# The value products of two attentions: one piece or two halves among the first jobs

## The reference

```python
def moba_nsa_mixer(h, w_in, w_out, rel_bias, cmp_pos_k, ...):       # layer 0: "first attention", EVEN
    mq, mk, mv, nq, kc, vc, ksl, vsl, kwn, vwn, gz = _split(hp @ w_in, EVEN_SPLITS)
    ...
    # 8 heads attend to their block of 256 keys, 8 more have three branches
    p_cmp = masked_softmax(s_cmp, ...); o_cmp = p_cmp @ v_cmp       # compressed keys
    o_slc = p_s @ v_s                                               # selected blocks
    o_win = p_w @ v_w                                               # window
    o_b = g[..., 0:1] * o_cmp + g[..., 1:2] * o_slc + g[..., 2:3] * o_win   # g = sigmoid(gz)
    return concat(o_a, o_b) @ w_out

def fox_mixer(h, w_in, b_forget, w_out):                            # layer 1: "second attention", ODD
    q, k, v, fz = _split(h @ w_in, ODD_SPLITS)
    cum = jnp.cumsum(jax.nn.log_sigmoid(fz + b_forget))
    p = masked_softmax(q @ k.T * scale + cq - cum, causal)
    return (p @ v) @ w_out                                          # 16 heads of 64
```

## Time and profile before

| | |
|---|---|
| time, median of 3 runs | 1239.46 us (1237.42 to 1242.24) |
| the profiled execution | 1237.19 us, of which its span 1235.4 us |
| PE busy | 1192.0 us (96% of the span), 7770 instructions |
| PEld busy | 1046.7 us (85%) |
| DVE busy | 825.7 us (67%) |
| ACT busy | 658.1 us (53%) |
| POOL busy | 236.0 us (19%) |
| granted TensorE clock | 0.995, in the mean |
| DMA | 205.56 MB in the span, mean 166 GB/s |

### The profile page before, as it was taken

How to read it: one execution, slowest core, us unless ns; L and a number is a source line. 1 busy time by engine, 2 the same in 40 slices (tenths; PEclk the granted TensorE clock), 3 DMA queues, 4 the chain that set the end, 5 groups by cost and what they waited for, 6 DMA issues and landing times.

```text
span 1235.4 us, 19213 instructions
## 1 busy us (share of the span) xinstructions
PE 1192.0 (96%) x7770; PEld 1046.7 (85%) x7770; DVE 825.7 (67%) x1267; ACT 658.1 (53%) x1074; POOL 236.0 (19%) x300
## 2 busy tenths in 40 slices
PE   7898999999999999999999999999999899999996
PEld 6786788888888688888888889999997698888996
DVE  5957776666586686675657777457865757667643
ACT  6428666643343756664346655336546754655531
POOL 4104421210000431220012222000004511212101
PEclk9999999999999999999999999999999899999999
DMA  7791245455444335455544554652451122455451
GB/s 281 253 240 35 102 171 197 181 202 204 173 171 194 148 105 202 174 201 205 190 171 153 202 182 152 205 213 105 171 205 69 35 103 104 170 197 178 158 196 56
DMA packets 33800, 205.56 MB, mean 166 GB/s; under 512 B 3744, under 2 KB 6320, under 8 KB 12720
## 3 DMA queue, kind: packets, MB, share of 16 engines
q1 hardware_dynamic: 30416, 200.47, 45.4%
q10 hardware_dynamic: 3296, 3.87, 1.6%
HBM read 202.87 MB, written 1.46 MB: 165 GB/s over the span
## 4 chain that ended last, share of the span: by engine, by line
PE 77%; DVE 13%; ACT 5%; DMA 2%; issue 1%; ACTq 0%; POOL 0%; POOLq 0%; DVEq 0%
PE ps L669 36%; PE ps L674 23%; PE ps L672 5%; PE ps L673 5%; DVE wl L611 4%; DMA e_bt<-scratch 2%; DVE tf L2228 1%; ACT wh L582 1%; PE ps L693 1%; PE ps L695 1%; PE ps L694 1%; DVE y L1949 1%; ACT pb L924 1%; DVE xb L747 1%; ACT pb L923 1%
## 5 line engine op out<-in xcount | busy, mean ns | idle before, releaser
L611 DVE TENSOR_TENSOR wl<-raw,wh 128x2048 fp32r<-128x2048 f32 (+2 forms) x194 | 420.4, 2172 | 148.3 <-ACT wh L582 148.3
L669 PE MATMUL ps<-xb,wh 128*128 128x512 f32 x1424 | 500.7, 397 | 4.6 <-DVE wl L611 4.1
L674 PE MATMUL ps<-xb,wl 128*128 128x256 f32 x1696 | 475.6, 280 | 0.0
L582 ACT ACTIVATE wh<-raw 128x2048 fp32r<-128x2048 f32 (+2 forms) x196 | 352.1, 1799 | 151.1 <-PE ps L674 112.9
L669 PEld LDWEIGHTS ps<-xb,wh 128*128 128x128 f32 x1424 | 267.3, 188 | 70.3 <-issue 5.7
L674 PEld LDWEIGHTS ps<-xb,wl 128*128 128x128 f32 x1696 | 321.6, 190 | 0.0
L674 PE MATMUL ps<-ab,wl 128*128 128x256 f32 x1088 | 305.7, 281 | 0.0
L669 PE MATMUL ps<-ab,wh 128*128 128x512 f32 x640 | 225.1, 397 | 0.1
L674 PEld LDWEIGHTS ps<-ab,wl 128*128 128x128 f32 x1088 | 206.4, 190 | 0.0
L669 PEld LDWEIGHTS ps<-ab,wh 128*128 128x128 f32 x640 | 120.1, 188 | 29.2 <-DVE ab L982 0.8
L866 DVE TENSOR_TENSOR tf<-ps,tf 128x256 f32<-128x256 f32 x148 | 61.8, 421 | 117.7 <-ACT tf L861 117.5
(11 more groups left out here) (324 smaller groups left out, 1324.7 us busy)
## 6 DMA issues: line engine op xcount, KB each, us to landing
raw<-wstream SPq DMA_DIRECT2D x162, 1024.0 KB, 4.8
raw<-wstream SPq DMA_DIRECT2D x32, 704.0 KB, 4.1
e_bt<-scratch ACTq DMA_DIRECT2D x16, 128.0 KB, 8.8
o_bt<-scratch SPq DMA_DIRECT2D x2, 1024.0 KB, 9.9
raw<-wstream SPq DMA_DIRECT2D x2, 560.0 KB, 8.8
raw<-wstream SPq DMA_DIRECT2D x4, 256.0 KB, 6.5
h<-xt ACTq DMA_DIRECT2D x4, 256.0 KB, 7.7
raw<-wstream SPq DMA_DIRECT2D x2, 512.0 KB, 9.7
```

Source lines behind the costliest of these rows:

```text
L582: e.g.activation(WH[i % HLN][:, 0:w], RAW[i % RAWN][:, 0:w], ACT.Copy).then_inc(S["hi"], 1)
L611: e.g.tensor_tensor(WL[q][:, 0:w], RAW[i % RAWN][:, 0:w], f32(WH[q][:, 0:w]), ALU.subtract).then_inc(S["lo"], 1)
L669: e.g.matmul(PS[b][:, :].rearrange("p (a t) -> p a t", a=2), wh[:, sl], x2[:, :, cs], start=start, stop=k == p.nk - 1, skip_group_check=pair)
L674: ins = e.g.matmul(o, wl[:, sl], xh[:, cs], start=False, stop=k == p.nk - 1, skip_group_check=pair)
```

## The change

What it does, by part:

- **First attention, PE.** `ev1` is done in two halves: chunk 14 in step 2 and chunk 15 in step 5, with scores 4 and 5 and turns 0 and 1 between them. Its outputs are in banks 1 and 0 (`fixed=(1, 0)`), those of the `pv` products.
- **First attention, ACT.** The high half of chunk 16 stands before exp 2; the copies of `ev1` and the gate exps stand in step 5 behind exp 5.
- **First attention, DVE.** The low half of chunk 16 stands in step 5, behind max 5, reciprocal 3 and the copy of turn 1. The factors' block of six instructions in steps 7 and 9 is cut in three: `dve_even_sums` in steps 1 and 2, `dve_even_gates` in 6 and 7, `dve_even_weights` in 8 and 9, with a semaphore `pcs` between them.
- **Second attention, PE.** `ov1` is done in two halves in steps 2 and 5 of the attention, into banks 1 and 0; `ov0` has banks 5 and 6.
- **Second attention, ACT and DVE.** The high half of chunk 65 stands in step 3, its low half in step 4; the copies of `ov1` behind exp 5. The quarters of chunk 66 move to ACT's steps 7, 9, 11, 13 and DVE's 14 to 17.
- **Banks.** Three products have no place in the ring any more, so later products take other banks than before.

The order in which SP fetches, and POOL's, are the same. The diff (the list of semaphores, which gains `pcs`, left out; so is the removal of `ov1` in front of the second attention on ACT and PE where a line only goes away):

```diff
@@ -290,7 +290,7 @@
         Gemm("kc", "small", 1, 0, 0, "ev_dve"), Gemm("vc", "small", 1, 0, 0, "ev_dve"),
         Gemm("ev0", "toks", 512, 8, 4, "ev_act"),
         Gemm("cs0", "small", 1, 0, 0, "ev_dve"), Gemm("cs1", "small", 1, 0, 0, "ev_dve"),
-        Gemm("ev1", "toks", 280, 8, 4, "ev_act"),
+        Gemm("ev1", "toks", 280, 8, 4, "ev_act", fixed=(1, 0)),
         Gemm("even", "attention", 0, 0, 0, ""),
         Gemm("eo", "cols", 8, 8, 16, "h_eo", fixed=(3, 4), wide=True),
         Gemm("up0", "cols", FF, 8, 16, "ev_dve", wide=True),
...
-        Gemm("ov0", "toks", 512, 8, 4, "ev_act"), Gemm("ov1", "toks", 512, 8, 4, "ev_act"),
+        Gemm("ov0", "toks", 512, 8, 4, "ev_act", fixed=(5, 6)), Gemm("ov1", "toks", 512, 8, 4, "ev_act", fixed=(1, 0)),
...
-        def pe_toks(e, p, ready):
+        def pe_toks(e, p, ready, part=slice(None)):
...
-            for _, k, c, at, fresh, signals in p.blocks:
+            for _, k, c, at, fresh, signals in p.blocks[part]:
...
@@ -1143,8 +1143,9 @@
             A = EVEN
             for i in range(A.n + 4):
                 if i == 2:
-                    act_exp_biased(e, A, 2)
-                    act_exp_biased(e, A, 3)
+                    hi_to(e, G["eo"].first)
+                if i == 5:
+                    act_exp_biased(e, A, 5)
                     act_gemm(e, G["ev1"], drain=act_toks(G["ev1"], e_v, 512, 0), ahead=1)
                     for tb in range(2):
                         gz = e_v[tb][:, 768:792]
@@ -1152,7 +1153,7 @@
                         e.g.activation(gz, gz, ACT.Exp, scale=-1.0).then_inc(S["gz"], 1)
                 if 9 <= i < 17 and i % 2:
                     hi_part(e, G["eo"].first + 1, (i - 9) // 2)
-                if i < A.n and i not in (2, 3):
+                if i < A.n and i != 5:
                     act_exp_biased(e, A, i)
                 if 0 <= i - 3 < A.n and i % 2:
                     act_turned(e, A, i - 3)
@@ -1272,8 +1273,12 @@
             for i in range(A.n + 5):
                 if i == 2:
                     dve_gemm(e, G["ev1"], 0, ahead=0)
-                if i in (7, 9):
-                    dve_even_gates(e, i // 9)
+                if i in (1, 2):
+                    dve_even_sums(e, i - 1)
+                if i in (6, 7):
+                    dve_even_gates(e, i - 6)
+                if i in (8, 9):
+                    dve_even_weights(e, i - 8)
                 if 16 <= i < 20:
                     lo_part(e, G["eo"].first + 1, i - 16)
                 if i == 12:
@@ -1284,11 +1289,13 @@
                     h = even_head(i)
                     e.wait_ge(S[f"bt{h // 8}"], 128)
                     dve_max_biased(e, A, i, e_bt[:, h * 256 + 128:h * 256 + 256], e_bt[:, h * 256:h * 256 + 256])
-                if i == 3:
+                if i == 5:
+                    dve_reciprocal(e, A, 3)
+                    dve_turned(e, A, 1)
                     lo_to(e, G["eo"].first)
-                if 0 <= i - 1 < A.n:
+                if 0 <= i - 1 < A.n and i != 4:
                     dve_reciprocal(e, A, i - 1)
-                if 0 <= i - 3 < A.n and i % 2 == 0:
+                if 0 <= i - 3 < A.n and i % 2 == 0 and i != 4:
                     dve_turned(e, A, i - 3)
                 if 0 <= i - 5 < A.n and even_last(i - 5):
                     d = even_pair(i - 5)
@@ -1296,16 +1303,24 @@
             dve_gemm(e, G["eo"], 1, drain=dve_residual(G["eo"], S["h_eo"], 1), between=behind_chunk(1))
 
         def dve_even_gates(e, tb):
-            gz, ss = e_v[tb][:, 768:792], SMALL[:, 16 + tb * 8:24 + tb * 8]
+            gz = e_v[tb][:, 768:792]
             e.wait_ge(S["gz"], tb + 1)
             e.link(e.g.tensor_scalar(gz, gz, 1.0, None, ALU.add))
             e.settle()
             e.g.reciprocal(gz, gz).then_inc(S["gated"], 1)
+
+        def dve_even_sums(e, tb):
+
+            ss = SMALL[:, 16 + tb * 8:24 + tb * 8]
             e.wait_ge(S["pce"], tb + 1)
             e.link(e.g.tensor_reduce(ss, pcv[:, tb, :, 0:15], AX, ALU.add))
             e.settle()
-            e.link(e.g.reciprocal(ss, ss))
-            e.settle()
+            e.g.reciprocal(ss, ss).then_inc(S["pcs"], 1)
+
+        def dve_even_weights(e, tb):
+
+            ss = SMALL[:, 16 + tb * 8:24 + tb * 8]
+            e.wait_ge(S["pcs"], tb + 1)
             e.wait_ge(S["gated"], tb + 1)
             e.link(e.g.scalar_tensor_tensor(out=ss, in0=ss, scalar=c_("valid")[:, tb:tb + 1],
                                             in1=e_v[tb][:, 768:792:3], op0=ALU.mult, op1=ALU.mult))
@@ -1389,8 +1404,8 @@
             A = EVEN
             pe_even_scores(e, 0)
             for i in range(A.n + 4):
-                if i == 2:
-                    pe_toks(e, G["ev1"], x_ready(0))
+                if i in (2, 5):
+                    pe_toks(e, G["ev1"], x_ready(0), slice(0, 4) if i == 2 else slice(4, 8))
                 if i == 12:
                     e.wait_ge(S["ol"], 3)
                     e.wait_ge(S["pct"], 2)
@@ -1638,13 +1653,16 @@
             softplus_act(e, o_lf[:, :], 32, 1)
             act_gemm(e, G["ok"])
             act_gemm(e, G["ov0"], drain=act_toks(G["ov0"], o_v, 0, 2))
-            act_gemm(e, G["ov1"], drain=act_toks(G["ov1"], o_v, 512, 2), ahead=1)
             A = ODD
             for i in range(A.n + 4):
-                if 1 <= i < 9 and i % 2:
-                    hi_part(e, G["oo"].first + 1, i // 2)
+                if 7 <= i < 15 and i % 2:
+                    hi_part(e, G["oo"].first + 1, (i - 7) // 2)
                 if i < A.n:
                     act_exp_biased(e, A, i)
+                if i == 3:
+                    hi_to(e, G["oo"].first)
+                if i == 5:
+                    act_gemm(e, G["ov1"], drain=act_toks(G["ov1"], o_v, 512, 2), ahead=1)
                 if 0 <= i - 3 < A.n and i % 2:
                     act_turned(e, A, i - 3)
                 q = i - 4
@@ -1666,11 +1684,13 @@
             e.wait_ge(S["cum"], 1)
             e.g.tensor_scalar(TMP[1][0:16, 0:T], PS[MISC][0:16, 0:T], -1.0, None, ALU.mult).then_inc(S["cq"], 1)
             dve_gemm(e, G["ov0"], 0)
-            dve_gemm(e, G["ov1"], 0, ahead=1)
+            dve_gemm(e, G["ov1"], 0, ahead=0)
             A = ODD
             for i in range(A.n + 5):
-                if 8 <= i < 12:
-                    lo_part(e, G["oo"].first + 1, i - 8)
+                if 14 <= i < 18:
+                    lo_part(e, G["oo"].first + 1, i - 14)
+                if i == 4:
+                    lo_to(e, G["oo"].first)
                 if i < A.n:
                     at = i % 8 * T
                     e.wait_ge(S[f"ct{i // 8}"], 16)
...
-            pe_toks(e, G["ov1"], x_ready(2))
             A = ODD
             pe_odd_scores(e, 0)
             for i in range(A.n + 4):
+                if i in (2, 5):
+                    pe_toks(e, G["ov1"], x_ready(2), slice(0, 4) if i == 2 else slice(4, 8))
```

2 lines of the change are left out of this document (1 added, 1 removed).

## The result

The changed kernel takes 1231.12 us in the median of 8 runs (1225.15 to 1235.82), the kernel before 1238.97 in 8 runs beside them (1234.73 to 1242.24): ratio 0.9933, 95% interval 0.991 to 0.9956. The profiled execution took 1231.03 us, its span 1229.2 after 1235.4. In two later comparisons the same kernel had ratios of 0.9966 (0.9941 to 0.999) and 0.994 (0.9919 to 0.9962).

What follows compares the result with a forecast made beforehand. PE was taken as the bound in both attentions, with 5.9 us idle there. Gains of 2.8 us (first) and 1.4 us (second) made 4.2, taken from the median 1239.46: 1235.3 us, range 1231.5 to 1240.0.

Steps and rivals of the forecast that it cites:

- the second attention's term: Second attention: 1.4 us gained, from 1.1 for POOL, 0.2 for the copies of `ov1` and 0.1 of ACT's waits.
- the first attention's term: First attention: 2.8 us gained, as 0.8 + 1.1 + 1.1 - 0.2 from waits for POOL, maxima and copies.
- The bound: Both attentions: PE is the bound, and its idle 3.94 and 1.93 us are all a better order can give.
- 0.1 of ACT's: Second attention: of PE's 0.5 us wait for ACT's copies, 0.1 was counted as gained.
- 0.8 for POOL: First attention, ahead of turn 2: the 0.97 us wait goes, 0.2 is left for POOL, so 0.8 gained.
- 2.2 for maxima and copies, less 0.2: First attention, factor block cut: 1.1 us from maxima, 1.1 from ACT's turned copies, minus 0.2 for DVE's copy.
- First value product with no slack: First attention, jobs 0 and 1: the value product meets the copies of `ev1` near 102.3, waiting 0 to 0.2 us.
- The rule weighed: First attention, job 3: DVE and POOL block each other for a whole instruction; weighting ends at 103.3, 0.1 before turn 3.
- my row: Profile row: POOL's pair of 0.99 us takes 1.42 beside DVE's low quarter; weighting of job 3 would end 0.4 later.
- The sum: Both attentions: 2.8 + 1.4 = 4.2 us gained.
- three runs' median moves by a us or more by itself: Whole kernel: scatter of the median of three runs, allowed for in setting the range 1231.5 to 1240.0.
- My chance of 0.12 for a gain above 0.5%: Whole kernel: 1233.3 us or less, by the case of full gain and the median's own scatter; chance 0.12.

Runs made afterwards that it cites:

- o_quarters: The kernel before with only the quarters of chunk 66 moved six steps later in the second attention, which took 51.46 us after 53.23.
- after: The changed kernel's first profile, with the whole change against the kernel before: profiled execution 1231.03 us, ratio 0.9933 in 8 runs.
- c_before: The kernel before once more, unchanged, as a measure of chance: ratio 1.0007 (0.9977 to 1.0037) in 12 runs.
- e_odd: The second attention's part of the change alone, the first attention as in the kernel before: ratio 1.000 (0.9974 to 1.0025).
- g_only: The kernel before with only DVE's factor block cut in three, run once: first attention 51.96 us.
- g_q: The kernel before with the factor block cut in three and the quarters of chunk 66 moved, both value products whole: ratio 0.9934 (0.9912 to 0.9955).
- c_after: The changed kernel once more, unchanged, as a measure of chance: ratio 0.9966 (0.9941 to 0.999) to the kernel before.
- e_even: The first attention's part of the change alone, the second attention as in the kernel before: ratio 0.9995 (0.997 to 1.002).

## Why the prediction was wrong

**The step that failed.** It is the second attention's term, 1.4 us, which measured 2.92: the quarters of chunk 66, priced at nothing, alone gave 1.77. The sum hides this in part, since the first attention's term was 0.6 to 1.0 us too high. The gain in time, 7.85 us, is larger than the 4.7 to 5.1 that the traces explain, and the lower bound of the range left too little room for the scatter of medians.

**The bound.** Right: PE is the bound in both attentions, and its idle time in the second, 1.97 us, went down to 0.07. The limit that I drew from it was wrong: "5.9 us is all that a better order can give" counts idle time only, and 1.02 of the 2.92 us came out of the time that is booked as busy.

**Second attention, 1.4 us.** The term was mis-sized: 2.92. I gave all of POOL's 1.1 and 0.2 for the copies, and "0.1 of ACT's". `o_quarters` shows what I had not priced: the quarters of chunk 66, which I took for a mere shift of a fetch, gave 1.77 us by themselves, 1.2 of it from DVE's quarters ahead of the maxima and 0.6 from ACT's first one. The halves give the other 1.15: no run has them alone, but turn 2 comes 1.13 us earlier in `after` than in `o_quarters`, and from there the two are alike. I had also read only the idle column. The turns, scores and values of a pair of jobs take 2.8 us where nothing holds them, and 3.3 to 3.45 where ACT was late behind DVE's maxima, of which only 0.23 is called idle. Three such turns before, and two after:

```profile
421.72 0.50 PE L916 MATMUL ps<-consts,pb 128*128 128x128 f32 x3
...
425.17 0.52 PE L916 MATMUL ps<-consts,pb 128*128 128x128 f32 x3 [0.23 <-ACT pt L942]
...
428.48 0.52 PE L916 MATMUL ps<-consts,pb 128*128 128x128 f32 x3 [0.23 <-ACT pt L942]
```

```profile
414.65 0.50 PE L916 MATMUL ps<-consts,pb 128*128 128x128 f32 x3
...
417.44 0.50 PE L916 MATMUL ps<-consts,pb 128*128 128x128 f32 x3
```

**First attention, 2.8 us.** 0.8 for POOL was a wait that stands in one execution of the kernel before and in none of the five other profiles with `ev1` whole and in its old place (`c_before`, `e_odd`, `o_quarters`, `g_only`, `g_q`): 0.85 of it goes with the late bias transfer of that execution, and a half-clock stretch hides the rest. Where it was not there, the halves gave 0.14 to 0.16 us. 2.2 for maxima and copies, less 0.2, was right as a sum, 1.95 for the cut block, but not in its parts: the maxima's 1.1 went, of ACT's waits 0.6 and not 1.1, DVE's copy stayed at 0.4, and the rest came out of the time booked as busy. Sum 1.8 to 2.2 in place of 2.8. For an execution with the late transfer and a full clock 0.8 may be right; no run of the changed kernel was one.

**First value product with no slack.** Not decided. With the half clock there are some 1.3 us of slack. For a full clock, which I had assumed, the estimate above takes a good part of them away. Of my start, max 0 at 93.21, 0.74 us were the wait for the bias transfer; in `after` max 0 comes 0.7 us earlier and the high half ends at 96.9 instead of 97.7.

**The rule weighed.** It did act, and I had its price right. In the changed kernel the weighting of job 3 meets the low half of chunk 16. First an undisturbed pair of POOL's instructions, then the second one of job 3, then what DVE did beside it:

```profile
98.06 0.82 POOL L972 TENSOR_SCALAR pb<-pb,rs 128x128 f32<-128x128 f32 x2 [1.80 <-DVE rs L966]
```

```profile
102.17 2.56 POOL L972 TENSOR_SCALAR pb<-pb,rs 128x256 f32<-128x256 f32 x1
```

```profile
102.10 2.28 DVE L611 TENSOR_TENSOR wl<-raw,wh 128x2048 fp32r<-128x2048 f32 x1
```

An instruction that takes 0.48 us otherwise (the longer one of the pair of 0.82) took 2.56 and ended 0.35 us after DVE's (2.56 in `c_after` too). So POOL stood still for as long as DVE's instruction ran, as the rule has it, and not for the 0.4 us of my row. It cost PE nothing: job 3 was weighted at 104.73, and turn 3 started at 105.79 with no wait.

**The sum.** At equal clock the attentions give 4.7 to 5.1 us where I had 4.2: two errors of opposite sign, so that it came this near is partly luck. That would be about 1234.5 on my scale, inside the range.

**The median and the range.** The other failed step is "three runs' median moves by a us or more by itself", which makes the lower bound 1231.5. Executions of one program differ by up to 17 us (1228.49 to 1245.39 for the kernel before in 71 runs): 3.1 us for a half-clock stretch of 6.8 us near 980, about 2.3 us for the pace of a product such as `up1`. Comparison by comparison the means differ by 7.7, 5.7 and 7.3 us; over all three they are 1232.1 (31 runs) and 1238.3 (71 runs): 6.3 us, give or take 1.5. The trace accounts for 4.7 to 5.1 of it. The rest, 1.2 to 1.6, stays open. It is not the half clock: the granted clock is 0.9927 in the mean of the 31 runs and 0.9925 in the 63 of before for which it is on record, 0.3 us of time, give or take 1.0. Whether it is chance, or the order has some influence on how often the slow pace comes, one profile for each kernel can't tell. The variants don't settle it: `e_even` and `e_odd`, at 0.9995 and 1.000, had less gain in time than in their traces, `g_q`, at 0.9934, more. My chance of 0.12 for a gain above 0.5% was too low with such a mean.

## What to carry to other kernels

Read the period of a pipeline in its timeline, start to start, and not only the idle column: a third of the 2.9 us that came back in the second attention had been booked as busy. The same timeline tells which engine's work is in the way, and here it was not the engine that PE's list names. PE waited for ACT's copies, ACT for DVE's maxima, and these stood behind DVE's quarters. Ask of every piece of work that stands ahead of such a step whether it could stand elsewhere; two such moves, of some lines, gave 1.9 and 1.8 us, most of the 4.7 to 5.1 of the whole change. And take the kernel before a second time before pricing a wait: one of 1.0 us, on which 0.8 of the sum rested, was there in one execution only, behind a transfer that was late once.

## What the hardware showed beyond that

- TensorE falls to half its clock for 3.4 or 6.8 us in 12 of 13 profiles, from a point between 90.2 and 92.9 us on, right after some 3 us of matmuls with 15 columns and while the scores or `ev1` run; the first profile of the kernel before has the same matmuls and no fall. Near 980 us it does so for 6.8 or 10.2 us in 11 of 13. These stretches and a last one of some 8 to 10 us at the very end are all that the granted clock of the whole span, 0.990 to 0.995 in the profiles, counts.
- At full granted clock a streamed product runs at one of two paces (L669: 399 or 394 ns a matmul, L674: 281 or 277; 703 matmuls of `up1` in 123.68 or 121.33 us). `up1` had the slow one in six of the 13 profiles, of kernels with either order, and the pace holds for most of a product. Nothing in the profile says what picks it.
